# The second layer's norm, four tiles of five, inside the first layer's expert steps

## What is computed

```python
for l in range(DEPTH):
    h = rms_norm(x, P['norm_mix'][l]) * (1 + sc1) + sh1
    out = even_mixer(h, ...) if l % 2 == 0 else odd_mixer(h, ...)
    x = x + g1 * out
    h = rms_norm(x, P['norm_ffn'][l]) * (1 + sc2) + sh2
    x = x + g2 * peer(h, P, l)
```

## Time and profile before

| | us |
|---|---|
| median of 3 runs (lowest to highest) | 4912.46 (4904.35 to 4913.8) |
| the profiled execution | 4908.48 |
| its span in the trace | 4906.7 |
| busy in the span: PE, DVE, POOL, ACT | 3926.7, 3116.1, 2672.7, 1051.3 |

### The profile page before, as it was taken

One profiled execution on the slowest core, in us unless ns is written; L12 is line 12 of the kernel. 1 busy time (PEld: TensorE's weight loads), 2 busy tenths in 40 slices (PEclk: granted clock), 3 DMA queues, 4 the chain that ended last, 5 costly groups with the idle time before them and its releaser, 6 DMA issues. The chain is left out here.

```text
span 4906.7 us, 41363 instructions
## 1 busy us (share of the span) xinstructions
PE 3926.7 (80%) x11732; PEld 1821.3 (37%) x11732; DVE 3116.1 (64%) x8304; ACT 1051.3 (21%) x2804; POOL 2672.7 (54%) x2872
## 2 busy tenths in 40 slices
PE   6596698887877977877789998688878779778777
PEld 2354473332322322322256666433323223223222
DVE  0123757777777677677336666487777776776774
ACT  1202241111111111111235554111111111111111
POOL 1010006777777677677532322067777777777775
PEclk9896799999999999999989999899999999999999
DMA  9910129999999999999821011189999999999998
GB/s 389 371 62 10 41 89 350 395 403 404 390 408 405 389 409 406 387 405 409 345 80 48 24 47 37 78 340 399 401 404 397 403 405 391 409 406 394 410 409 347
DMA packets 456205, 1508.39 MB, mean 307 GB/s; under 512 B 50838, under 2 KB 99894, under 8 KB 455228
## 3 DMA queue, kind: packets, MB, share of 16 engines
q0 software_dynamic: 371104, 1347.37, 69.6%
q1 hardware_dynamic: 80284, 141.82, 8.0%
q10 hardware_dynamic: 4608, 16.78, 0.8%
HBM read 1484.84 MB, written 20.94 MB: 307 GB/s over the span
## 5 line engine op out<-in xcount | busy, mean ns | idle before, releaser
L627 PE MATMUL psall<-work 128*128 128x512 f32 x5120 | 2440.9, 608 | 652.5 <-DMA work<-in_p_v,idx 587.8
L435 DVE CUSTOM_DVE_ANT_0 work<-work,psall 128x1024 f32<-128x1024 f32 x1280 | 1518.5, 1218 | 846.2 <-DMA work<-in_p_u,idx 846.2
L348 POOL DMA_INDIRECT work<-in_p_u,idx x1280 | 1213.8, 948 | 923.0 <-DVE idx L413 449.9
L627 PEld LDWEIGHTS psall<-work 128*128 128x128 f32 x5120 | 890.3, 189 | 2198.1 <-issue 1119.4
L356 POOL DMA_INDIRECT work<-in_p_v,idx x1280 | 1217.0, 951 | 494.3 <-issue 321.5
L536 ACT ACTIVATE work<-ident,work 128x128 f32<-128x128 f32 x1280 | 487.4, 399 | 1933.9 <-PE psall L627 1897.6
L1407 PE MATMUL psall<-work 128*128 128x512 f32 x640 | 283.0, 595 | 9.0 <-ACT work L1499 5.2
L574 PE MATMUL psall<-work 128*128 128x512 f32 x640 | 278.3, 592 | 0.0
L574 PEld LDWEIGHTS psall<-work 128*128 128x128 f32 x640 | 121.6, 190 | 153.1 <-issue 153.1
L1407 PEld LDWEIGHTS psall<-work 128*128 128x128 f32 x640 | 119.1, 191 | 144.7 <-issue 144.7
L1380 POOL TENSOR_SCALAR work<-work 128x256 f32<-128x256 f32 x40 | 33.8, 845 | 238.5 <-ACT work L1491 238.5
(11 more groups left out here) (274 smaller groups left out, 3725.3 us busy)
## 6 DMA issues: line engine op xcount, KB each, us to landing
work<-in_w_ada SPq DMA_DIRECT2D x64, 768.0 KB, 12.4
work<-in_p_u,idx POOLq DMA_INDIRECT x1280, 8.2
work<-in_p_v,idx POOLq DMA_INDIRECT x1280, 8.3
work<-in_o_w_in SPq DMA_DIRECT2D x40, 512.0 KB, 7.0
work<-in_p_w_qT SPq DMA_DIRECT2D x32, 512.0 KB, 13.8
wqk_rows<-work ACTq DMA_DIRECT2D x32, 512.0 KB, 7.4
work<-wqk_rows SPq DMA_DIRECT2D x2, 6144.0 KB, 20.1
work<-mod_rows SPq DMA_DIRECT2D x16, 512.0 KB, 5.6
```

What stands on the lines that cost most here:

```text
L348: nc.gpsimd.indirect_dma_start(m.ur[:, b, :], None, u_flat, bass.IndirectOffsetOnAxis(ap=e, axis=0)).then_inc(s.ud[b].h, 16)
L435: nc.vector.tensor_tensor_reduce(m.ur[:, b, :], m.ur[:, b, :], m.h2p[:, :], 1.0, 0.0, ALU.mult, ALU.add, m.d16[:, j:j + 1]).then_inc(s.ufr ...
L627: q = nc.tensor.matmul(o[:, k * 512:(k + 1) * 512], m.dgb[:, j % DIAGS, :], m.vr[:, b, k * 512:(k + 1) * 512], start=(i == 0 and j == 0), ...
```

## The change

The second layer's norm is split. Tiles 0 to 3 are normed in the first layer's expert block, during the last tile's steps 33 to 37; `norm_phase` of the second layer is called with tile 4 alone and does not load the four rows, which SP now loads in the expert block after the last scores. `early` maps step 33 + t to tile t. The addition of the shift is DVE's in the early tiles, not POOL's. The transposes go through PSUM banks 6 and 7, which serve as the scratch of the early statistics too. (`range(TILES)` replaces the old loops in the first layer, where nothing changes.)

```diff
+    early = {} if out else {(TILES - 1) * PH + 1 + t: t for t in range(TILES - 1)}
...
+            if early:
+                sp.wait_ge(s.pqp.h, s.pqp.at(4 * TILES))
+                for c in range(2):
+                    for k in range(2):
+                        sp.dma_start(m.bc[:, c, k, :], m.mod[l * 12 + 12 + 6 * c + k:l * 12 + 13 + 6 * c + k, :].to_broadcast([P, D])).then_inc(bcs[c].h, 16)
...
+            def normed_early(t):
+                c = cond_of(t)
+                dve.wait_ge(bcs[c].h, bcs[c].at(32))
+                dve.wait_ge(s.rs.h, s.rs.at(t + 1))
+                if t >= 1:
+                    dve.wait_ge(s.tp.h, s.tp.at(t))
+                ch(nc.vector.scalar_tensor_tensor(out=m.ph[:, :], in0=x[:, t, :], scalar=m.rs[:, t:t + 1], in1=m.bc[:, c, 0, :], op0=ALU.mult, op1=ALU.mult))
+                nc.vector.tensor_tensor(m.ph[:, :], m.ph[:, :], m.bc[:, c, 1, :], ALU.add).then_inc(s.hs.h, 1)
...
                 if i == 2 and t >= 1:
                     added(t - 1)
+                if g - 1 in early:
+                    normed_early(early[g - 1])
...
+            def statistics_early(t):
+                act.wait_ge(s.accfree.h, s.accfree.at(t + 1))
+                if t >= 1:
+                    act.wait_ge(s.tpfree.h, s.tpfree.at(t))
+                ch(nc.scalar.activation(m.junkA[:, :], x[:, t, :], ACT.Square, accum_out=m.ss[:, t:t + 1]))
+                ch(nc.scalar.activation(m.ss[:, t:t + 1], m.ss[:, t:t + 1], ACT.Ln, scale=1.0 / D, bias=m.eps[:, 0:1]))
+                nc.scalar.activation(m.rs[:, t:t + 1], m.ss[:, t:t + 1], ACT.Exp, scale=-0.5).then_inc(s.rs.h, 1)
+
+            def turned_early(t):
+                act.wait_ge(s.tp.h, s.tp.at(t + 1))
+                for b in range(2):
+                    q = nc.scalar.activation(m.hT[:, 4 * b:4 * b + 4, t * P:(t + 1) * P], ps[6 + b][:, :].rearrange("p (c t) -> p c t", c=4), ACT.Copy)
+                q.then_inc(s.tpfree.h, 1)
...
+                if g in early and early[g] == 0:
+                    statistics_early(0)
...
                 if i == 3 and more:
                     turned(t + 1)
+                if g - 1 in early:
+                    turned_early(early[g - 1])
+                    if g in early:
+                        statistics_early(early[g])
...
+            def turn_early(t):
+                pe.wait_ge(s.hs.h, s.hs.at(t + 1))
+                for k in range(KC):
+                    q = nc.tensor.transpose(ps[6 + k // 4][:, (k % 4) * P:(k % 4 + 1) * P], m.ph[:, k * P:(k + 1) * P], m.ident[:, :])
+                q.then_inc(s.tp.h, 1)
...
+                if g - 1 in early:
+                    turn_early(early[g - 1])
...
-    norm_phase(nc, m, 1, 0, first_weights)
+    norm_phase(nc, m, 1, 0, first_weights, range(TILES - 1, TILES))
```

More of the change, by code:

```diff
@@ L225, in _, with norm_phase @@
             ch.close()
-def norm_phase(nc, m, l, which, prefetch):
+def norm_phase(nc, m, l, which, prefetch, tiles):
     s = m.sems
@@ L237, in _ @@
         def _(sp):
-            for c in range(2):
+            for c in range(2 if 0 in tiles else 0):
                 for k in range(2):
@@ L249, in _ @@
             ch = Chain(act, s.ca)
-            for t in range(TILES):
+            for t in tiles:
                 ch(nc.scalar.activation(m.ph[:, :], x[:, t, :], ACT.Square, accum_out=m.ss[:, t:t + 1]))
@@ L281, in _ @@
         def _(pe):
-            for t in range(TILES):
-                pe.wait_ge(s.hr.h, s.hr.at(t + 1))
+            for t in tiles:
+                pe.wait_ge(s.hr.h, s.hr.at(t + 1 - tiles[0]))
                 if t >= 2:
@@ L291, in norm_phase @@
         q.base += 32
-    for q in (s.rs, s.tp, s.tpfree, s.hr, s.hs):
+    for q in (s.rs, s.tp, s.tpfree, s.hs):
         q.base += TILES
+    s.hr.base += len(tiles)
 def router_weights(m, sp, l):
@@ L312, in project_and_peer @@
     STEPS = TILES * PH
+    bcs = (s.bc, s.bc1)
+    early = {} if out else {(TILES - 1) * PH + 1 + t: t for t in range(TILES - 1)}
     def bank(t):
@@ L769, in first_weights @@
         sp.dma_start(m.wrow[CONV:CONV + 1, :], m.e_conv_b).then_inc(s.wl.h, 16)
-    norm_phase(nc, m, 0, 0, first_weights)
+    norm_phase(nc, m, 0, 0, first_weights, range(TILES))
     with nc.Block() as block:
```

## The result

The changed kernel takes **4920.27 us** (median of 20 runs) against 4910.31 us before (20 runs): +10.0 us, ratio 1.0019 with a 95% interval from 1.0013 to 1.0026. One execution of each twenty was far longer (10098.77 us before, 5566.94 us after); the medians are over all twenty, the ratio is without these two. The forecast was 4921, with a range from 4908 to 4930, and +9 for the change.

The account below looks back on a forecast made before the run. Expert steps were taken as DMA-bound while POOL has gathers queued, the seam as bound by SP's transfer list. The terms -6 + 2 + 1.7 + 11.2 gave +9 us, forecast 4921 us, range 4908 to 4930.

Parts of the forecast that it names:

- The new wait of DVE, steps 35 to 37, +11.2: DVE waits 3.65 us for ACT's statistics in each of three expert steps, delaying POOL's ninth u gather: 11.2 us lost.
- POOL was to stand idle 6 us or more ahead of the ninth gather: Sign of being right: in steps 35 to 37 POOL idles 6 us or more before its ninth u gather.
- No slack at 14.7 us: Expert steps: 41.4 us leaves 14.7 us from the previous L526 to the ninth gather, with no slack left.
- Step 34, +1.7: DVE's scaling and adding, 2.46 us, move the ninth gather from 14.9 to 17.3 us: 1.7 us lost.
- the broadcasts, +2: Four row broadcasts moved into the expert phase compete with the gathers for DMA: 2 us lost, between 0 and 5.1.
- The seam, -6, set by SP's list: Between the layers SP's transfers, not the norm, set the end; four broadcasts fewer gain 6 us, at least 1.75.
- Rival D: The seam follows the norm after all and falls by 20 us; sum -5, or -16 with A; chance 0.04.
- Rival A: Not slower: DVE's wait does not become time in steps 35 to 37; -2 to -4 us, about 4909; chance 0.16.
- Rival B: Dearer holes: longer queue refill, no room for broadcasts, slow weight loads; +19 us, 4932, anything above +14; chance 0.08.
- Rival C: POOL's port decides: POOL issues beside DVE's norm take 0.9 us longer; +12.6 us, 4925; chance 0.08.
- The median against the profiled execution: Profiled 4908.48 us gives 4917.5 with the change; the median of the runs shown is 4.0 above: forecast 4921.

Follow-up runs that it names:

- experiment 1: Changed kernel with ACT's statistics of tiles 0 to 2 at the head of step 33, tile 3's at step 35: 4910.1 us.
- experiment 2: Changed kernel with the Square of the statistics of tiles 1 to 3 done three times over: 4926.6 us.
- experiment 4: Of the change only the four early broadcasts kept, all five tiles normed between the layers: 4907.8 us, ratio 0.9999 against the kernel before.
- experiment 5: Changed kernel with the second head's five weight loads and the two gate broadcasts moved from the seam into the next block: 4906.0 us.
- experiment 6: Kernel before the change, with the second head's five weight loads and two gate broadcasts moved from the seam into the next block: 4907.1 us.
- experiment 7: Changed kernel with unused PE transposes added in the seam, 60 plus 90, then 60 plus 130: 4919.9 and 4922.1 us, single runs.
- experiment 3: Changed kernel with statistics ahead and DVE's scaling and adding behind the tenth dot product, one step earlier: 4907.6 us.

## Why the prediction was right

- *The new wait of DVE, steps 35 to 37, +11.2.* +11.44, of the foreseen place and kind. DVE waited 3.9 us, not 3.65 (the prediction's own rows give 4.95 - 1.33 = 3.62); the ninth gather left at 18.7, not 18.5 us; what follows it took 26.3 to 27.1 us, against 26.7. Experiments 1 and 2 move the time with the wait in both directions: shown. One sign was missed: POOL was to stand idle 6 us or more ahead of the ninth gather, and it was 5.04 us in each of steps 34 to 37, the first of them without this wait, so POOL's idle time does not measure it.
- *No slack at 14.7 us.* Nearly: in experiment 1 the ninth gather leaves at 15.7 us and the steps take 42, about half a microsecond each over before. From 18.7 us (45.2) to 21.0 us (47.7) it is one for one.
- *Step 34, +1.7; the broadcasts, +2.* +1.72, with the ninth gather at 17.3 us as forecast; and +2.01 in the profiled execution, 0.6 to 2.0 us over the traces (experiment 4).
- *The seam, -6, set by SP's list.* -5.78; experiments 4 to 6 show the list. Rival D falls: without the list, and only then, the seam follows the norm.
- *Rival A* falls by the 11.7 us of waits, though its premise was sound: with the statistics there in time all but 1.6 of the 11.44 us are gone. *Rival B*: nothing was dearer than the sum; a median 10 us over before, where B begins at 14. *Rival C*, POOL's port: its 0.8 us stand ahead of an idle of 5.04 us, and in experiment 1 the steps with such an issue came out below a sum that leaves it out.
- *The median against the profiled execution.* The profiled run before was 4.0 below the median of the three runs shown; over 20 runs it is 1.8 (4910.31 - 4908.48). The forecast of +9 was a little low (the median says 10.0) and its base a little high, and the two offset each other: that forecast and median are only 0.7 us apart is partly luck.

Not tried: an earlier load of the first head's weights, for which PE still waits 3.5 us in experiment 5; they lie on v buffers that the last step reads.

## What to carry to other kernels

Ask of each stage which list ends last before moving work out of it: four fifths of a norm left the seam, and the seam ended with a list of loads of which half were not needed at once. Work moved into a full loop costs by where it stands in each engine's list, not by its length: the same 2.5 us on DVE cost 3.8 us a step behind a chain over three engines ahead of the first dot product, and nothing between the later ones. And the head of a step is another moment for each engine, so an operand made "a step ahead" may still come last.

## What was not expected of the hardware

- PE's clock fell inside the expert steps too: granted 0.89 in step 35 of the changed kernel, in which PE stands idle once for 3.3 and once for 3.8 us, and 1.00 in the same step of experiment 1, with the same work and no idle time over 1.7 us. No cost of it shows: what follows the ninth gather took 26.4 us there, and 26.3 in step 3 of the kernel before.
- In experiment 7 the clock stayed at 1.00 over 2.2 us of idle PE behind 130 transposes and fell within 5.3 us of idle PE behind 90 (0.69 on average over them). The full speed of 2.4 GHz comes back some microseconds into the first projection, later in some runs than in others (11.22 to 12.88 us to the second). The Trainium skill, TensorE: Matmul & The Clock Gate, "Part 1: The HAM clock gate", says that the low clock is the default and activity lifts it; the trace agrees, with 9.83 us against 11.2 to 12.9.
- A POOL issue that starts while DVE scales a tile ends 2.1 us after the scaling's start (starts 0.34, 0.69 and 0.96 us into it took 1.76, 1.41 and 1.14 us in the changed kernel), but two in experiment 3 that start 0.02 and 0.03 us into it took 0.94 us, as usual. The Trainium skill, SBUF — State Buffer, "SBUF: two separate sides", says that of the two the one that starts first holds the shared port for its whole length and the other waits. For the issue the trace agrees: the scaling takes 1.28 us, and 0.8 us of the issue come after it. For the scaling it does not: in step 36 of the changed kernel an issue of 0.94 us starts 0.56 us ahead of the scaling, which takes its 1.28 us all the same, and the measurement decides.
